# A decoder trunk on one Trainium2 core: where the rotated state-space products of the second chunk are added

## What is computed

```
bu_re = jnp.einsum('blgh,gph->lbgp', u, bb_re)
bu_im = jnp.einsum('blgh,gph->lbgp', u, bb_im)
_, _, s_re, s_im = lax.associative_scan(_complex_affine_combine, (a_re, a_im, bu_re, bu_im), axis=0)
y = (jnp.einsum('lbgp,ghp->blgh', s_re, c_re) - jnp.einsum('lbgp,ghp->blgh', s_im, c_im))
y = jax.nn.gelu(y + d_skip * h)
z = y @ w_glu
val, gate = jnp.split(z, 2, axis=-1)
return val * jax.nn.sigmoid(gate)
...
def chunk_fn(args):
    hc, ic, gc = args
    act = jnp.einsum('cd,ckd->ck', hc, u_tab[ic])
    return jnp.einsum('ck,ckd->cd', gc * jax.nn.gelu(act), v_tab[ic])
```

## Time and profile before

| | us |
|---|---|
| median of 3 runs (1774.82 to 1781.13) | 1778.36 |
| profiled execution, own time | 1774.45 |
| its span | 1772.7 |
| PE busy, share of the span | 72% |
| DVE busy | 63% |
| ACT busy | 38% |
| POOL busy | 35% |
| DMA, mean over the span | 387 GB/s |
| state-space loop of the second chunk, first rotation to first GLU matmul | 218.1 to 386.4 |

### The profile page before, as it was taken

The page is one execution under the profiler, slowest core; times in us unless marked ns, Lnnn a source line. Parts: engine busy times, 40 slices in busy tenths (PEclk is TensorE's granted clock), DMA queues, the critical chain, the costliest instruction groups (busy, mean ns, idle before and its releaser), DMA issues.

```text
span 1772.7 us, 17526 instructions
## 1 busy us (share of the span) xinstructions
PE 1283.5 (72%) x5714; PEld 538.4 (30%) x5714; DVE 1116.2 (63%) x2512; ACT 675.5 (38%) x2012; POOL 623.9 (35%) x557
## 2 busy tenths in 40 slices
PE   4784455577966977997777699789987974555554
PEld 2471111122711323333245133353352720000000
DVE  8959888973648756445446766543553677677544
ACT  7624422222233338117323431751382243233222
POOL 4213343532233224334323232332332344444441
PEclk9997578889967999998889699899998987876878
DMA  8069999999997999999999899999999999999997
GB/s 329 9 247 382 382 414 407 410 413 423 424 413 281 427 423 420 424 426 420 423 424 421 332 375 423 421 357 425 421 381 414 421 353 420 415 419 414 420 421 302
DMA packets 86636, 685.81 MB, mean 387 GB/s; under 512 B 9872, under 2 KB 10256, under 8 KB 12176
## 3 DMA queue, kind: packets, MB, share of 16 engines
q0 software_dynamic: 73728, 536.90, 73.9%
q1 hardware_dynamic: 12816, 147.79, 19.9%
HBM read 683.60 MB, written 1.05 MB: 386 GB/s over the span
## 4 chain that ended last, share of the span: by engine, by line
DMA 34%; PE 33%; DVE 19%; ACT 7%; issue 5%; POOL 2%; another core or an unknown queue 0%; SPq 0%; POOLq 0%; ACTq 0%; DVEq 0%
DMA ringmem<-experts,lay 21%; PE ps L456 12%; PE ps L412 10%; DMA wt<-w_qkv 8%; DVE ringmem L1155 6%; PE ps L468 5%; POOL ringmem L1126 2%; DMA wt<-w_o 2%; PE ps L427 2%; ACT S L758 2%; DMA wt<-w_q 1%; PE ps L660 1%; ACT lay L816 1%; PE ps L635 1%; ACT L753 1%
## 5 line engine op out<-in xcount | busy, mean ns | idle before, releaser
L1126 POOL DMA_INDIRECT ringmem<-experts,lay x512 | 592.5, 1157 | 1072.5 <-PE ps L412 939.2
L412 PE MATMUL ps<-ringmem,S 128*32 128x512 f32 x2048 | 619.4, 765 | 389.7 <-ACT S L758 384.6
L1155 DVE CUSTOM_DVE_ANT_0 ringmem<-ringmem,Hrep 128x1024 f32<-128x1024 f32 x512 | 613.8, 1223 | 295.4 <-DMA ringmem<-experts,lay 279.0
L412 PEld LDWEIGHTS ps<-ringmem,S 128*32 128x32 f32 x2048 | 114.7, 127 | 804.9 <-ACT S L758 546.0
L753 ACT ACTIVATE gelus<-dots 128x2 f32<-128x2 f32 x256 | 51.6, 201 | 663.7 <-DVE dots L1155 655.2
L456 PE MATMUL ps<-wt,hT 128*128 128x512 f32 x576 | 256.2, 598 | 14.8 <-DMA wt<-w_qkv 14.6
L456 PEld LDWEIGHTS ps<-wt,hT 128*128 128x128 f32 x576 | 106.5, 190 | 164.6 <-issue 159.1
L749 ACT ACTIVATE S<-con,lay 128x32 f32<-128x32 f32 x512 | 134.3, 310 | 44.1 <-PE ps L412 44.1
L758 ACT ACTIVATE S<-S,gelus 128x32 f32<-128x32 f32 x512 | 136.6, 314 | 24.9 <-ACT gelus L753 1.5
L468 PEld LDWEIGHTS ps<-hT,wt 128*128 128x128 f32 x1024 | 116.8, 194 | 12.5 <-issue 7.2
L468 PE MATMUL ps<-hT,wt 128*128 128x128 f32 x1024 | 119.3, 278 | 1.0 <-DMA wt<-w_q 1.0
(11 more groups left out here) (199 smaller groups left out, 1115.8 us busy)
## 6 DMA issues: line engine op xcount, KB each, us to landing
wt<-w_qkv SPq DMA_DIRECT2D x36, 2048.0 KB
wt<-w_q SPq DMA_DIRECT2D x16, 2048.0 KB
wt<-w_glu SPq DMA_DIRECT2D x5, 2048.0 KB, 12.9
ringmem<-experts,lay POOLq DMA_INDIRECT x512
wt<-w_o SPq DMA_DIRECT2D x4, 2048.0 KB
ringmem<-w_glu SPq DMA_DIRECT2D x3, 2048.0 KB, 21.6
gain<-gains SPq DMA_DIRECT2D x9, 512.0 KB
area<-keys SPq DMA_DIRECT2D x4, 1024.0 KB, 9.6
```

The costliest lines, as they stand in the source:

```text
L412: last = pe.matmul(ps[TG * t:TG * (t + 1), half, :], S[:, u % 2, i, :], ring[:, (2 * u + i) % RING, D + half * 512:D + (half + 1) * 512], ...
L1126: pool.indirect_dma_start(ring[:, s % RING, :], None, experts[phase // NC], bass.IndirectOffsetOnAxis(ap=rows[:, phase % NC, j, n:n + 1], ...
L1155: last = v.tensor_tensor_reduce(ring[:, i, 0:D], ring[:, i, 0:D], Hrep[:, j, :], 1.0, 0.0, ALU.mult, ALU.add, dots[:, b, second:second + 1])
```

## The change

It concerns only the second chunk (`c` = 1). DVE's rotation no longer adds: it writes four products, cos*re (T1), cos*im (T3), sin*im (T2) and -sin*re, the last into P1, and adds the carried state into T1 and T3. PE gets a new step `s5_sum(k)`: with the 128x128 identity as weights it passes T1 and T2 into one PSUM group of 512 columns (bank 3), and T3 and P1, in two halves of 256 columns, into the upper halves of banks 4 and 5. DVE's scans read their input there: one scan of 512 columns, two of 256 (`sum_ready`). As P1 is now written in the rotation, the rotation waits for `y_ready` of the step before ahead of that product. bu(k) waits for `scanned` in place of `bu_used`. DVE's places become: rotate(k), pairs 4k and 4k+1, scan(k), pairs 4k+2 and 4k+3. PE's sum(k) stands behind pair 4k. ACT's, POOL's and SP's orders stay.

```diff
             def s5_bu(c, k):
                 u = KT * c + k
                 if k >= 1:
-                    pe.wait_ge(bu_used, u)
+                    pe.wait_ge(*((scanned, k) if c else (bu_used, u)))
...
+            def s5_sum(k):
+
+                pe.wait_ge(rot_ready, k + 1)
+                if k:
+                    pe.wait_ge(scanned, k)
+                for i, t in enumerate((T1, T2)):
+                    pe.matmul(ps[:, 3, :], ident, t.rearrange("p q t -> p (q t)"),
+                              start=(i == 0), stop=(i == 1), skip_group_check=True)
+                for h in range(2):
+                    for i, t in enumerate((T3, P1)):
+                        last = pe.matmul(ps[:, 4 + h, 2 * P:4 * P], ident,
+                                         t[:, 2 * h:2 * h + 2, :].rearrange("p q t -> p (q t)"),
+                                         start=(i == 0), stop=(i == 1), skip_group_check=True)
+                last.then_inc(sum_ready, 1)
...
                 for k in range(KT):
+                    if c:
+                        g.at(gphase, S5_AT + S5_K * k + 1)
+                        s5_sum(k)
                     g.at(gphase, S5_AT + S5_K * (k + 1) - 1)
...
                 v.tensor_tensor(T1, co, bre, ALU.mult)
+                v.tensor_tensor(T3, co, bim, ALU.mult)
                 v.tensor_tensor(T2, si, bim, ALU.mult)
-                link(v.tensor_tensor(T3, si, bre, ALU.mult))
-                link(v.tensor_tensor(T1, T1, T2, ALU.add))
-                v.tensor_tensor(T2, co, bim, ALU.mult).then_inc(bu_used, 1)
+                v.wait_ge(y_ready, u)
+                v.scalar_tensor_tensor(out=P1, in0=si, scalar=-1.0, in1=bre, op0=ALU.mult,
+                                       op1=ALU.mult).then_inc(bu_used, 1)
                 v.wait_ge(bu_used, u + 1)
-                link(v.tensor_tensor(T2, T2, T3, ALU.subtract))
...
-                link(v.tensor_tensor_scan(flat[3], flat[0], flat[1], 0.0, ALU.mult, ALU.add))
-                v.tensor_tensor_scan(flat[4], flat[0], flat[2], 0.0, ALU.mult, ALU.add).then_inc(scanned, 1)
-                v.wait_ge(scanned, k + 1)
+                v.wait_ge(sum_ready, k + 1)
+                flat = [t.rearrange("p q t -> p (q t)") for t in (MS, zr, zi)]
+                link(v.tensor_tensor_scan(flat[1], flat[0], ps[:, 3, :], 0.0, ALU.mult, ALU.add))
+                for h in range(2):
+                    cols = slice(2 * P * h, 2 * P * (h + 1))
+                    last = v.tensor_tensor_scan(flat[2][:, cols], flat[0][:, cols], ps[:, 4 + h, 2 * P:4 * P], 0.0,
+                                                ALU.mult, ALU.add)
+                last.then_inc(scanned, 1)
...
-                        g.at(gphase, S5_AT + 1)
+                        g.at(gphase, S5_AT)
...
-                    g.at(gphase, S5_AT + S5_K * k + 1)
+                    g.at(gphase, S5_AT + S5_K * k + 2)
```

More of the change, by code:

```diff
@@ L250, in build @@
         bu_used = sem("bu_used")
+        rot_ready = sem("rot_ready")
+        sum_ready = sem("sum_ready")
         prod_ready = sem("prod_ready")
@@ L1250, in s5_rotate @@
                 u = KT * c + k
-                if u:
-                    v.wait_ge(prod_ready, u)
+                v.wait_ge(prod_ready, u)
                 v.wait_ge(bu_ready, u + 1)
@@ L1257, in s5_rotate @@
                 v.tensor_tensor(T1, co, bre, ALU.mult)
+                v.tensor_tensor(T3, co, bim, ALU.mult)
                 v.tensor_tensor(T2, si, bim, ALU.mult)
-                link(v.tensor_tensor(T3, si, bre, ALU.mult))
-                link(v.tensor_tensor(T1, T1, T2, ALU.add))
-                v.tensor_tensor(T2, co, bim, ALU.mult).then_inc(bu_used, 1)
+                v.wait_ge(y_ready, u)
+                v.scalar_tensor_tensor(out=P1, in0=si, scalar=-1.0, in1=bre, op0=ALU.mult,
+                                       op1=ALU.mult).then_inc(bu_used, 1)
                 v.wait_ge(bu_used, u + 1)
-                link(v.tensor_tensor(T2, T2, T3, ALU.subtract))
-                for src, z0 in ((T1, z0re), (T2, z0im)):
+                for src, z0 in ((T1, z0re), (T3, z0im)):
                     last = v.tensor_tensor(src[:, :, 0:1], src[:, :, 0:1],
                                            z0[:, PPT * k:PPT * (k + 1)].unsqueeze(2), ALU.add)
-                link(last)
+                last.then_inc(rot_ready, 1)
             def s5_scan(c, k):
                 u = KT * c + k
-                zr, zi = T3, T1
+                zr, zi = T1, T2
                 v.wait_ge(ms_ready, k + 1)
-                flat = [t.rearrange("p q t -> p (q t)") for t in (MS, T1, T2, zr, zi)]
-                link(v.tensor_tensor_scan(flat[3], flat[0], flat[1], 0.0, ALU.mult, ALU.add))
-                v.tensor_tensor_scan(flat[4], flat[0], flat[2], 0.0, ALU.mult, ALU.add).then_inc(scanned, 1)
-                v.wait_ge(scanned, k + 1)
+                v.wait_ge(sum_ready, k + 1)
[6 more added lines that the diff above has]
+                last.then_inc(scanned, 1)
                 co, si = tile_of(cosT, k), tile_of(sinT, k)
@@ L1281, in s5_scan @@
                 v.tensor_tensor(P2, si, zr, ALU.mult)
+                v.wait_ge(scanned, k + 1)
                 v.scalar_tensor_tensor(out=P3, in0=si, scalar=-1.0, in1=zi, op0=ALU.mult, op1=ALU.mult)
```

## The result

| | before | changed |
|---|---|---|
| median, us | 1779.74 (4 runs, 1774.82 to 1783.93) | 1819.32 (4 runs, 1815.41 to 1823.50) |
| profiled execution, own time | 1774.45 | 1823.50 |
| first rotation to first GLU matmul | 218.1 to 386.4 | 218.7 to 425.3 |
| one step of the loop | 20.54 | 25.64 |

The change makes the kernel slower: ratio 1.0229, 95% interval 1.0205 to 1.0254, some 40 us. The profiled execution of the changed kernel is the slowest of its four, so its 49 us over before overstate the difference by some 9.

What follows compares the result with a forecast made beforehand. The loop was taken as close to the DMA's limit (410 of 424 GB/s). Steps of 28.5 us for 20.54 made the loop +61, less 13 given back, net +48 on 1774.45: 1822, put at 1824 us, range 1790 to 1846.

Steps and rivals of the forecast that it cites:

- The wait for the sum: DVE ahead of its first scan: sum ready 10.6 us after the rotation, 4.6 covered, a new wait of 6.0 a step.
- Pair 4k+2 at 3.63: PE's pair ahead of bu: after long idle time it runs at the low clock and takes 3.63 us.
- bu to DVE 1.34: Handover from PE to DVE: DVE's rotation starts 1.34 us after bu.
- The rotation at 4.7 us: DVE's rotation: P1 waits some 1.9 us for a late `y_ready`, so 4.7 us instead of 2.8.
- rival C: DVE's rotation: `y_ready` comes with the end of y, rotation 2.8 us, kernel 1811 us; chance 0.13.
- The step, 28.5: One changed loop step, from scan to scan along what is waited for: 28.5 us against 20.54.
- The loop, +61 us: Loop up to the first GLU matmul: it starts at 447.6 against 386.4, 61 us later.
- Given back, 13 us: Behind the loop: DMA queues start empty in GLU and the stage after it, returning 13 us.
- B: PE in the loop: both pairs stay at 2.4 GHz, 27 us less, kernel 1797 us; chance 0.14.
- D: PE in the loop: the sum runs at 1.2 GHz, 28 us more, kernel 1852 us; chance 0.08.
- E: Loop: DVE's 1.6 us a step count, sum hidden behind two pairs, DMA binds; faster, 1773 to 1769; chance 0.04.
- GB/s in the loop: Sign to look for: the DMA's rate in the loop falls from 410 to about 300 GB/s.

Runs made afterwards that it cites:

- e2: The changed kernel with PE's sum moved ahead of pair 4k instead of behind it; ratio to before 0.9983, step 20.43 us.
- second profile: The changed kernel, unaltered, run and profiled again beside two other kernels; ratio to before 1.0250, step 26.83 us.
- e5: The changed kernel with the sum ahead of pair 4k and bu and y behind pair 4k+1; ratio to before 0.9960, step 19.91 us.
- e1: The kernel before with only DVE's places moved as in the change, no sum on PE; ratio 1.0036, step 21.84 us.
- e3: The changed kernel with T2 and P1 left out of the sum, output wrong; ratio to before 1.0139, step 23.81 us.
- e7: The kernel before with PE's bu and y one pair later, behind pair 4k+3; ratio 1.0112, step 23.73 us.
- e4: The kernel before with PE's bu and y behind pair 4k instead of pair 4k+2; ratio 0.9981, step 20.01 us.

## Why the prediction was right, and where it was not

The sign, the place and the size in the whole hold: 1819 measured, 1824 forecast. Two terms were wrong, the length of the loop (+61 for +39 us in the first profile) and what is given back behind it (13 for some 3 at most), and they nearly cancel. That the total came out within 5 us is in part luck.

- **The wait for the sum, 6.0 us a step**: 5.5 on average in the first profile, 5.74 to 5.93 in six of its eight steps, and 6.6 on average in the second. Right, and e2 shows that it is the place: one pair earlier and the loss is gone. Pair ahead of the sum, sum and hop were put at 3.63 + 3.55 + 0.1 = 7.3; the rows have 258.14 - 250.84 = 7.3, but split as 2.8 and 4.5, and 5.7 in the two short steps. In five steps of the second profile pair and sum together took 8.3 to 8.5. The sum met the low clock in part: in the first 3.0 us of one sum of the second profile the granted clock was 0.62 of full speed, behind a pair at 0.50 (1.2 GHz); in the short step it was 1.00 (2.4 GHz) for both. The first two rows are of the second profile, the others of the first; the third number from the end is the clock:

```profile
304.50:308.00 3.50, 3.50 (x8) 0.52 (x8) 1.35 (x4) 1.08 (x5) 0.00 (x0) 0.50 0.98 396
308.00:311.00 3.00, 3.00 (x7) 1.42 (x6) 0.00 (x0) 0.54 (x2) 1.87 (x2) 0.62 1.02 358
...
277.13:279.00 1.87, 1.87 (x9) 0.41 (x9) 1.37 (x4) 0.74 (x4) 1.04 (x1) 1.00 0.96 302
279.00:282.60 3.60, 3.60 (x14) 2.16 (x12) 0.00 (x0) 0.79 (x4) 1.88 (x2) 1.00 0.99 387
```

- **Pair 4k+2 at 3.63 and bu to DVE 1.34**: 3.63 in the step shown (3.24 in one other), and 269.81 to 271.18 = 1.37. Right. That every pair behind 3.6 us or more of idle PE takes 3.6 was read a little too widely: in the kernel before some took 3.4.
- **The rotation at 4.7 us: wrong, and the mis-sized step.** It took 271.18 to 273.84 = 2.66. In the first profile P1 never waited: L1280 starts 1.80 after L1276, and ACT's gelu 1.49 after it. In the second it waited in five of eight rotations, 2.5 us in all, where the term had 1.9 in every step. So this was rival C, to which I gave 0.13, wholly in one profile and for the most part in the other. The seven waits of ACT were real, but I carried a delay over from one order of PE's work to another without knowing its cause, and in the new order it was absent or short. The rule of the Trainium skill that was set against it ("TensorE: Matmul & The Clock Gate", "The mechanism": matmuls finish in order), read with the modelled end, gave the right time in the first profile, where `y_ready` came 0.07 us behind it. In the second it came 0.7 to 1.9 behind, and in the kernel before 2.0 to 3.4. Nothing here shows matmuls out of order, and nothing shows true ends.
- **The step, 28.5**: 25.64 and 26.83 in two profiles. Of the 2.86 that are missing from the first, 2.04 are the rotation, 0.4 the two short steps, the rest scans (4.83 for 4.95) and links.
- **The loop, +61 us**: +38.8 (425.26 against 386.44); in the second profile +49.5.
- **Given back, 13 us: wrong.** Some 3 us came back in GLU, and in the first profile they were lost again. The four GLU projections start at 386.44, 397.04, 406.40 and 417.20 before and at 425.26, 434.10, 443.72 and 452.77 now, so the lag went from 38.8 to 35.6:

```profile
417.20 7.13 PE L456 MATMUL ps<-wt,gT 128*128 128x512 f32 x16 [1.83 <-DMA wt<-w_glu]
...
452.77 7.13 PE L458 MATMUL ps<-wt,gT 128*128 128x512 f32 x16
```

The first of these rows is the kernel before, the second the changed one. At the spreading of the next phase's rows the lag was 39.3 again (557.23 against 517.91), and the medians differ by 39.6. In the second profile it was 49.5 us at the first projection, 46.8 at the fourth (464.02) and 46.3 at the first projection of layer 1 (611.80 against 565.50). By the end of its span the first profile had lost another 10 (1821.7 against 1772.7), the second next to nothing (1819.7). The working took the queue of one gather for a debt of the DMA. What counts is bytes: the loop of before moved 168.3 x 410 = 69.0 MB, that of the change 206.6 x 340 = 70.2 MB, so the DMA was ahead by 1.2 MB, some 3 us, when GLU began, and about as much came back in GLU. The ring is filled only as PE frees it; the last pairs are freed at the loop's end in both kernels, and right behind it DVE waits for a gather (4.12 us here, 3.59 for one at 402.69 in the kernel before):

```profile
429.71 1.23 DVE L1175 CUSTOM_DVE_ANT_0 ringmem<-ringmem,Hrep 128x1024 f32<-128x1024 f32 x1 [4.12 <-DMA ringmem<-experts,lay]
```

- **The rivals.** B (both pairs at full clock) fails for pair 4k+2, 3.63 in the step shown, and holds for pair 4(k+1) only in the short steps. D (sum at the low clock) holds in part: 4.4 to 4.7 for 3.55 in four steps of the first profile, 4.6 to 4.8 in five of the second. E was excluded rightly for this order, but e2 and e5 show that its mechanism (DVE's saving, the sum hidden, the DMA binding) is what the same arithmetic does with the sum one pair ahead.
- **GB/s in the loop** was to fall to about 300; it fell to 340, with the shorter loop (69.0 MB / 206.6 us = 334).

## What to carry to other kernels

Where two engines have fixed orders, a helper step that one makes for the other belongs directly behind its input, not behind a piece of streaming work that itself waits for the engine being helped: the same six matmuls cost 2.5% behind that pair and nothing ahead of it. Before work is moved off a busy engine, look for its idle time and for the stream underneath: here DVE idled 1.4 us a step on average for one matmul group's place, moving that group gained as much as moving the arithmetic, and the DMA was the floor for both. A delay read in the old order may belong to that order; as long as its cause is not known, it is a rival with a chance and not a term of the sum. And what a slow stretch gives back later is counted in bytes moved by its end, not in the queue of the last transfer.

## What the runs showed of the hardware

- The modelled end of a group of matmuls can be 2 to 4 us earlier than the semaphore behind it is seen. ACT, which waited only for `y_ready`, started 0.06 to 0.08 us behind y's modelled end in e1, e2, e3 and one profile of the change, 0.7 to 1.9 us in the other profile of the same kernel, 2.0 to 3.4 before, and 1.6 to 4.1 in e7. The start on the waiting engine is the witness.
- The same kernel had steps of 25.64 and 26.83 us in two profiles. A pair and the sum behind it took together 5.7 us at a granted clock of 2.4 GHz throughout, and 8.5 with the pair at 1.2 GHz and part of the sum too.
- With 16 DMA engines 0.88 busy the loop moved 340 GB/s; divided by the share that is 386, against 417 in e4 (421 at a share of 1.01). In these two rows the engines moved less also while they counted as busy; why is open.
- A scan of 512 columns took 1.22 us from PSUM and from SBUF alike.
